# Spreading the front of a streamed transformer layer over other slots of its expert stream, with consumers moved further behind their producers

## What is computed

```
h = rmsnorm(x, g_norm1);  z = h @ w_in
o_gla, S_new = gla_recurrence(gq, gk, gv, log_a, S0)      # gated linear attention, chunks of 64
o_fox = fox_attention(rmsnorm(fq), rmsnorm(fk), fv, c_all, P)   # softmax attention with a forget gate
x = x + concat(rmsnorm(o_gla) * silu(gg), o_fox) @ w_out
h2 = rmsnorm(x, g_norm2)
q = (h2 @ w_q).reshape(.., 8 heads, 2, 128)
s1, i1 = top_k(q[.., 0] . subkeys, 16);  s2, i2 = top_k(q[.., 1] . subkeys, 16)
top, ti = top_k(s1[.., :, None] + s2[.., None, :], 16)     # 16 of 256 pairs, for each head
idx = i1[ti // 16] * 128 + i2[ti % 16];  g = softmax(top)
a = gelu(u_tab[idx] . h2)                                  # 8 x 16 = 128 experts for each frame
x = x + sum((g * a) * v_tab[idx])
```

## Time and profile before

| | |
|---|---|
| median of 3 runs | 3522.37 us (3512.01 to 3527.95) |
| the profiled execution | 3523.86 us, of which its span is 3522.1 us |
| mean granted TensorE clock | 0.876 of full |
| busy | PE 78%, DVE 73%, ACT 43%, POOL 36% |
| moved by DMA | 1287.09 MB, 365 GB/s over the span |

### The profile page before, as it was taken

How to read it: one execution, slowest core, us unless ns; L and a number is a source line. 1 busy time by engine, 2 the same in 40 slices (tenths; PEclk the granted TensorE clock), 3 DMA queues, 4 the chain that set the end, 5 groups by cost and what they waited for, 6 DMA issues and landing times. The chain is left out here.

```text
span 3522.1 us, 33822 instructions
## 1 busy us (share of the span) xinstructions
PE 2743.5 (78%) x9149; PEld 1604.5 (46%) x9149; DVE 2567.4 (73%) x5555; ACT 1500.5 (43%) x3900; POOL 1270.4 (36%) x1070
## 2 busy tenths in 40 slices
PE   7858878777887886777878887767887788777767
PEld 5736545333654453334644454334553445333322
DVE  1286655898668877887668777887667767888775
ACT  2343354444324744443236644444235553444433
POOL 0023312333343443333434443323333434444343
PEclk9979978988898998987988898888998989888899
DMA  8498957999998999998999999878998999999998
GB/s 307 171 346 344 392 210 295 373 345 351 370 421 342 398 415 393 346 335 340 422 411 341 411 410 415 334 297 358 422 421 317 405 357 418 421 421 406 362 410 365
DMA packets 189479, 1287.09 MB, mean 365 GB/s; under 512 B 24184, under 2 KB 25992, under 8 KB 37608
## 3 DMA queue, kind: packets, MB, share of 16 engines
q0 software_dynamic: 153360, 1112.08, 79.2%
q1 hardware_dynamic: 31160, 166.84, 11.9%
q10 hardware_dynamic: 4768, 6.00, 0.5%
HBM read 1262.74 MB, written 22.10 MB: 365 GB/s over the span
## 5 line engine op out<-in xcount | busy, mean ns | idle before, releaser
L1279 PE MATMUL ps_acc<-uv_ring,coef_diag 128*128 128x512 f32 x2648 | 1512.5, 713 | 644.6 <-ACT coef_diag L970 630.3
L697 POOL DMA_INDIRECT uv_ring<-in_peer_uv,expert_index x1056 | 1260.2, 1193 | 2046.7 <-PE ps_acc L1279 1807.1
L1631 DVE CUSTOM_DVE_ANT_0 uv_ring<-uv_ring,h_rows 128x1024 f32<-128x1024 f32 x1056 | 1281.2, 1220 | 418.9 <-DMA uv_ring<-in_peer_uv,expert_index 412.8
L1279 PEld LDWEIGHTS ps_acc<-uv_ring,coef_diag 128*128 128x128 f32 x2648 | 561.0, 224 | 1359.7 <-ACT coef_diag L970 810.2
L965 ACT ACTIVATE gelu_u_dot_h<-u_dot_h 128x2 f32<-128x2 f32 x528 | 107.2, 203 | 1278.4 <-DVE u_dot_h L1631 1277.0
L1639 DVE SCALAR_TENSOR_TENSOR v_sums<-uv_ring,coefficients,v_sums 128x1024 f32<-128x1024 f32 x394 | 505.2, 1282 | 41.0 <-ACT coefficients L972 41.0
L1061 PE MATMUL ps_scores<-weight_chunk,rows_T 128*128 128x256 f32 x1728 | 418.3, 399 | 11.0 <-DMA weight_chunk<-in_w_in_chunks 11.0
L1061 PEld LDWEIGHTS ps_scores<-weight_chunk,rows_T 128*128 128x128 f32 x1728 | 347.6, 202 | 104.1 <-issue 41.6
L1250 PE MATMUL ps_scores<-weight_chunk,rows_T 128*128 128x256 f32 x1152 | 267.7, 387 | 2.2 <-DMA weight_chunk<-scratch_keys_w 1.4
L970 ACT ACTIVATE coef_diag<-coef_diag,gelu_u_dot_h 128x128 f32<-128x128 f32 x662 | 251.1, 398 | 17.5
L1250 PEld LDWEIGHTS ps_scores<-weight_chunk,rows_T 128*128 128x128 f32 x1152 | 224.9, 195 | 68.5 <-issue 38.4
(11 more groups left out here) (193 smaller groups left out, 2213.1 us busy)
## 6 DMA issues: line engine op xcount, KB each, us to landing
weight_chunk<-in_w_in_chunks SPq DMA_DIRECT2D x60, 1024.0 KB, 9.0
weight_chunk<-scratch_keys_w SPq DMA_DIRECT2D x40, 1024.0 KB, 9.0
weight_chunk<-in_w_out_chunks SPq DMA_DIRECT2D x20, 1024.0 KB, 9.0
uv_ring<-in_peer_uv,expert_index POOLq DMA_INDIRECT x1056, 11.2
uv_ring<-in_w_peer_q_T SPq DMA_DIRECT2D x8, 1024.0 KB, 9.2
rows_T<-in_x_T SPq DMA_DIRECT2D x9, 512.0 KB, 5.9
x_mid<-in_x_rows SPq DMA_DIRECT2D x9, 512.0 KB, 10.0
scratch_xm<-x_mid SPq DMA_DIRECT2D x9, 512.0 KB, 12.8
```

What stands on the lines that cost most here:

```text
L697: pool.indirect_dma_start(out=ring[:, s % RING, :], out_offset=None, in_=dram["uv"], in_offset=bass.IndirectOffsetOnAxis(ap=idx[:, t % IDX ...
L1279: mm = pe.matmul(acc[:, c, :], diag[:, r, :], ring[:, r, D + c * 512:D + (c + 1) * 512], start=first, stop=False, skip_group_check=True)
L1631: dve.tensor_tensor_reduce(out=ring[:, s % RING, 0:D], in0=ring[:, s % RING, 0:D], in1=h2[:], scale=1.0, scalar=0.0, op0=ALU.mult, op1=ALU ...
```

## The change

Three things change; what is computed, the data moved and the number of slots do not.

1. `front_plan` has other weights (0.3 for light steps, 2.1 for a projection unit, 1.36 for a GLA step, 1.6 for an output unit, 0.5, 0.37 for a routing step; attention gets 12.0 + 3.7 t for tile t, divided by its steps) in place of 0.6, 3.7, 1.1, 3.5, 1.5, 0.45 and 13.0 + 7.5 t. `BESIDE` now tells three kinds of stage apart.
2. `on_vector` gives VectorE one row of every two beside the projections, attention and output (three of four while the slot is below 128), one of four beside GLA as before, and three rows of sixteen beside routing, where it was one of four.
3. In `route` and in `attend` the consumers stand further back. A routing unit has its copy at step 10, the chain from 14, the index conversion at 21, the exponential at 25, the reciprocal of its sum (now `inverse`, no longer inside `router`) and the indices at 29, the weights at 32; a unit's last step is counted at 33 (`UNIT_ENDS`), 19 before. In `attend` each operation stands `lag(t)` steps behind the one that it needs: 2 for tiles 0 to 3, else 1 as before. Attention has `att_steps(t)` steps, 42 for tiles 0 to 3 and 32 or 33 for the others, where all had 33.

```diff
@@ front_plan @@
-        weight += [0.6] * (n + 1) + [3.7] * (IN_CH * n) + [0.6] * 2
+        steps(n + 1, PREP, MIXING)
+        steps(IN_CH * n, UNIT_IN, MIXING)
+        steps(2, PREP, MIXING)
...
-                due.append((base + UNIT * m + UNIT + 3, SLOTS * t + slots_of(t) // PH * j))
+                due.append((base + UNIT * m + UNIT_ENDS, SLOTS * t + slots_of(t) // PH * j))
@@ on_vector @@
-    return 1 if BESIDE[GRP * g + GRP] else g % 2
+    stage = BESIDE[GRP * g + GRP]
+    if stage == MIXING:
+
+        return 1 + g % 2 if GRP * g < SLOTS else 1
+    return g % 2 if stage == LINEAR else int(g % 8 in (1, 3, 6))
@@ attend, on each engine @@
-            for n in range(ATT_STEPS):
+            for n in range(att_steps(t)):
-                h, r = divmod(n - 4, 3)
+                h, r = divmod(n - 4 * lag(t), 3)
-                    hh, rr = divmod(n - 6 - q // 2, 3)
+                    hh, rr = divmod(n - 6 * lag(t) - q // 2, 3)
@@ route, ScalarE @@
-                m, r = divmod(step - 2, UNIT)
+                m, r = divmod(step - SCORES_AT, UNIT)
...
-                m, r = divmod(step - EXP_AT - 4, UNIT)
+                m, r = divmod(step - NUMBER_AT, UNIT)
+                if r == 0 and 0 <= m < PH * len(ts):
+                    j, i = divmod(m, len(ts))
+                    act.wait_ge(picked, base + m + 1)
+                    number(ts[i], j)
+                m, r = divmod(step - WEIGH_AT, UNIT)
                 if r == 0 and 0 <= m < PH * len(ts):
                     j, i = divmod(m, len(ts))
                     act.wait_ge(pin_r, base + m + 1)
                     weigh(ts[i], j)
-                    act.wait_ge(picked, base + m + 1)
-                    number(ts[i], j)
@@ route, VectorE @@
-            dve.wait_ge(tex, n + 1)
-            wait(dve, weighed, n)
-            dve.reciprocal(pinv[:], psum_[:]).then_inc(pin_r, 1)
...
+        def inverse(n):
+            dve.wait_ge(tex, n + 1)
+            wait(dve, weighed, n)
+            dve.reciprocal(pinv[:], psum_[:]).then_inc(pin_r, 1)
```

More of the change, by code:

```diff
@@ L137, in route_steps, with lag, value_at, att_steps @@
 def route_steps(ts):
-    return UNIT * PH * len(ts) + 4
+    return UNIT * (PH * len(ts) - 1) + UNIT_ENDS
+def lag(t):
+    return 2 if t < 4 else 1
+def value_at(t):
+    return 7 * lag(t) + 3 * (FH - 1) + (quads(t) - 1) // 2
+def att_steps(t):
+    return value_at(t) + 3 * lag(t) + 1
 def key_blocks(t):
@@ L219, in front_plan @@
         upto.append(max(f for f in range(len(total)) if total[f] <= at_work + 1e-6))
-    beside = [f < len(on_pe) and on_pe[f] for f in upto]
+    beside = [kind[f] if f < len(kind) else ROUTING for f in upto]
     return first, upto, len(weight), beside
@@ L1168, in attend @@
                     tr.then_inc(q_t, 1)
-                h, r = divmod(n - 2, 3)
+                h, r = divmod(n - 2 * lag(t), 3)
                 if r == 0 and 0 <= h < FH:
@@ L1178, in attend @@
                 for q in range(nq):
-                    hh, rr = divmod(n - 5 - q // 2, 3)
+                    hh, rr = divmod(n - 5 * lag(t) - q // 2, 3)
                     if rr == 0 and 0 <= hh < FH:
@@ L1189, in attend @@
                         value(t, hh, q)
-                if n == ATT_STEPS - 2:
+                if n == value_at(t) + 2 * lag(t):
                     pe.wait_ge(o_n, t + 1)
@@ L1483, in attend @@
             i = PLACE[t][1]
-            for n in range(ATT_STEPS):
-                h, r = divmod(n - 3, 3)
+            for n in range(att_steps(t)):
+                h, r = divmod(n - 3 * lag(t), 3)
                 if r == 0 and 0 <= h < FH:
```

53 lines of the change are left out of this document (33 added, 20 removed).

## The result

The changed kernel takes 3300.97 us (median of 4 runs, 3298.82 to 3302.15), the kernel before 3517.61 us (4 runs). The ratio is 0.938, with a 95% interval of 0.9355 to 0.9406: 6.2% less. The forecast was 3351 us, range 3290 to 3450. One of all the runs in this document was slow, 8717.61 us at a granted clock of 0.459 for the kernel with the old plan and the new lags: it counts in that kernel's median, 3384.23 us (3382.94 without it), but in no ratio.

What follows compares the result with a forecast made beforehand. Stages alternate between VectorE-heavy ones leaving bandwidth unused and ones held by bytes. Terms 191.5 + 83 + 583 + 720 + 757 + 520 + 496, plus 1.8 us outside the span, less 1.5 to the median, give 3351 us; range 3290 to 3450.

Steps and rivals of the forecast that it cites:

- What bounds the kernel: Whole program: stages asking much of VectorE leave bandwidth unused, the others are held by bytes, at most 422 GB/s.
- The surcharge on each need: Projections and attention: stage time taken as 1.07 times the largest need; routing as 1.05 times its bytes.
- Routing: Batch 3's routing: 95 slots, bytes 264 us, VectorE 255, lags remove its larger waits; 278 us, from 270.7.
- The first 20 slots: Start of the gather stream: 80.8 us as before plus two dots of 1.30 us, 83 us.
- Batch 1 as a whole: Sum of batch 1's stages, with 179 slots instead of 163: 583 us, from 607.3.
- Batch 1's attention: Held by neither TensorE nor VectorE; longer lag gives between 98 us (worth nothing) and 63 (all waits), taken as 75.
- Batch 4's attention: Batch 4's attention: TensorE's 210.8 us less 8 rows of 2.28 us, times 1.07, 206 us.
- Ahead of slot 0: Prologue: 23 more steps cost some 3 us, tile 0's lag gives that back; left at 191.5, bounds -15 and +10.
- Rival 1: Routing: the loop of gather, dot, weights and add holds; 3.2 us a slot instead of 2.93, 3430 us; chance 0.15.
- Rival 2: Projections, attention, output: TensorE has room, so they fall to their bytes without the 1.07, 3260 us; chance 0.08.
- Rival 3: Projections, attention, routing: TensorE's mean clock falls to 0.75 and its needs grow, 3563 us; chance 0.07.
- Rival 4: Whole program: 365 GB/s is the most gathers get over a long time, nothing moves, 3522 us; chance 0.04.

Runs made afterwards that it cites:

- the two experiments on the split: Changed kernel with the old rule for which engine adds a row, 3326.4 us; changed kernel with all rows beside routing on TensorE, 3295.27 us.
- cache_split: Changed kernel, but the sample tile's cached values have their own semaphore, so its first scores wait only for cached keys and gates: 3285.97 us.

## Why the prediction was right

The sign held, the time lay in the range, and the mechanism held in the main: 3351 forecast, 3301 measured, a gain of 6.2% instead of 4.9%. Against the sum, the stages came out as follows.

| stretch | forecast | measured |
|---|---|---|
| ahead of slot 0 | 191.5 | 192.6 |
| first 20 slots | 83 | 72.4 |
| batch 1 | 583 | 584.6 |
| batch 2 | 720 | 705.0 |
| batch 3 | 757 | 732.3 |
| batch 4 without routing | 520 | 514.4 |
| the last 184 slots | 496 | 498.4 |

- **What bounds the kernel.** Right. The taken ceiling of 422 GB/s was reached in batch 3's projections and output (421), and its routing and GLA rose from 342 and 340 to 413 and 385 GB/s.
- **The surcharge on each need (1.05 to 1.07).** This is the term that was too large, 25 us in batch 3 and 15 in batch 2. I carried the ratios of the kernel before over to the new one. By their own rates and times the new stages of batch 3 moved 301.5 MB, 714 us at 422 GB/s, and took 732.3, which is 1.025 times. Single stages can't be set against my sums so closely: the projections issued 53 gathers in their 50 slots, so they moved 65.8 MB where I had 62.8, and GLA moved 38.3 where I had 41.9. GLA's 99.5 us, which look like the 99 of my sum, are thus 1.10 times its own bytes.
- **Routing.** The price was 278 us at 92% VectorE busy; measured 271.4 at 93% in batch 3 and 271.7 in batch 2. The reason was partly right. The waits for copied key scores went, as forecast. But the stage ended at its bytes, and the two experiments on the split show that VectorE's 255 us were no bound at all.
- **The first 20 slots.** I priced them at the old rate plus two dots and gave them no part of the lags, though they are a routing stage like the others. That missed 10.6 us. With the new plan and the old lags they take 82.4 us, so it was the lags.
- **Batch 1 as a whole.** That 583 met 584.6 is luck. The projections (106 priced, 111.6 measured) and GLA (81, 87.0) took 12 us more, and routing (279, 268.6) took 10 less.
- **Batch 1's attention.** Priced at 75 us between 63 and 98, measured 75.1; undoing the lag gives 92.2. The lag's worth was judged rightly, the match to 0.1 us is luck: I had the stage held by nothing but waits, and at a higher clock the same code takes 68.1.
- **Batch 4's attention.** Priced at 206, measured 215.2. I took it for a stage of TensorE and bytes and overlooked that the denser order draws the first scores of tile 8 towards a load that can't start before tile 7's last product. That is a wait of 18.9 us, 5.6 before, and taking it out gives 15.
- **Ahead of slot 0.** 23 more steps and the lag of tile 0 together changed it by 1.1 us. That is no measurement of either: with the same code ahead of slot 0 it took 192.6 us in the change and 185.9 in `cache_split`.
- **The two parts.** Nowhere did I say what the lags are worth alone. They are the larger half, 132 us against 90.

The rivals. Rival 1 (the loop holds, a routing slot near 3.2 us) is out: 2.86 us in batch 3. Without the new lags it would have come near, 3.07 to 3.16 us a slot. Rival 2 (TensorE has room) fared better than its chance of 0.08. Its price, 3260, is 41 us off, the forecast 50. Its mark, projections under 152 us, was missed, but because they moved 3 MB more than my sum had: batch 3's run at 421 GB/s, which is the bytes' limit and not TensorE's, while those of batches 2 and 4 stay at 404 and 410. In routing, rows on TensorE cost nothing. The Trainium skill (Perfetto Trace Analysis, Identifying the Most-Contended Engine) says that a matmul's busy share is no good measure of how near TensorE is to its peak, and names the busy share of weight loads as one of the two better ones. The routing stage without rows on VectorE agrees: TensorE is busy 234 of 271 us, its weight loads 123, and it takes 18 rows more than in the change without lengthening the stage. Rival 3 (the clock falls) went the other way: the mean granted clock rose from 0.876 to 0.914. In one stage, batch 1's attention, the clock does cost time, as shown above. Rival 4 is refuted by 390 GB/s over the whole span and 421 over the 156 us of batch 3's projections.

The prediction took 358 GB/s from the Trainium skill (Perfetto Trace Analysis, Engine Utilization) as a limit for this kernel. The same section says that on trn2 this is one core's share when both cores of a pair use the memory, and that a core active alone can pull more, up to about 435 GB/s. The traces agree with that: one core ran, and it moved 421 to 422 GB/s in its fullest stages.

## What to carry to other kernels

When a stream with a small buffer runs beside stages of unlike needs, bandwidth left unused in one stage is lost: take each stage's need per engine and its bytes from the profile and give each stage as many slots as make its largest need equal to the time of its bytes. In a program of in-order queues, look for the one wait on the engine that holds the stage, and put its producer early enough; waits of the other engines can stay, and a second measure against the same wait brings little. After making an order denser, look again at the loads whose start depends on the end of a stage.
